# A hybrid decoder step on one core: triangular inverse in 64-blocks, an unlooped TensorE queue, and a reordered recurrence front

## The chip, the cores and the metric

One NeuronCore of a Trainium2 chip. The metric is the time of the whole program on the device, in microseconds, median of several executions. Five engines work side by side: TensorE (PE; PEld is its weight load), VectorE (DVE), ScalarE (ACT), GpSimd (POOL) and SyncE (SP, which issues DMAs). Each runs its own list of instructions in order and waits on semaphores for the others.

## What is computed

One layer step for a prompt of 512 tokens and 8 sampled tokens (520 columns in all), width 2048. Everything is fp32.

```python
xn = rms_norm(x, norm_w)
z  = xn @ w_in                       # 2048 x 8384: r, k, v, two LoRA inputs, gate | q, k, v, gate
# group A, 16 RWKV-7 heads of 64
zs = zs + mu * (zs_prev - zs)        # token shift
w  = exp(-exp(-0.5) * sigmoid(w0 + tanh(wd) @ w_up));  a = sigmoid(a0 + ad @ a_up)
kk = k * k_k / max(|k * k_k|, eps);  k = k * (1 + (a - 1) * k_a)
S_t = S_{t-1} diag(w_t) - (S_{t-1} kk_t) (kk_t a_t)^T + v_t k_t^T;   y_t = S_t r_t
y  = group_norm(y) + sum(r * k * r_k) * v       # the last term is the bonus
# group B, 16 heads of 64: QK-norm, ALiBi, three dilated windows merged by their denominators
out = x + concat(y * silu(g_r), o_att * silu(g_a)) @ w_out
```

For the prompt the recurrence is done in chunks of 128 tokens. Within a chunk it needs the inverse of a unit lower triangular 128x128 matrix I + N for each head, which is built by doubling: the inverse of 2x2 blocks, then 4x4, up to 128x128.

## The kernel before

**Stages.** A start (norm, transposes, LoRA inputs, the projection of pair 0), then 8 passes of `pair_a` (two RWKV heads each, pairs 0 to 7), 8 passes of `pair_b` (two attention heads each), then 8 passes of the output projection. While a pass works on its heads, TensorE also multiplies the input projection of the next pass: 64 *units* of six matmuls with 260 columns (`multiply_unit`, L443), 4 output tiles of 16 units. The tables `BEHIND_A` and `BEHIND_B` say after which step how many units are put into TensorE's queue (`fill`); `spread` gives the last step what is left over. The weights of a projection pass come in 8 half-tiles (8 units each): SP loads one, ScalarE rounds it (`round_half`, L419), GpSimd subtracts to get the rest (`rest_half`, L427), and unit u waits, where u is a multiple of 8, for half-tile u/8. ScalarE and GpSimd issue rounding and rest of half-tile k+1 at the unit 8k+1, at that unit's place in their own order of steps.

**Order.** Each engine's order is written by hand, as a list of named steps (`Steps`); a wait names a step of another engine. On TensorE, `pair_a` and `pair_b` are loops over seven passes, with the last pass written out behind the loop; the output passes 1 to 7 are a loop too.

**The front of `pair_a`.** TensorE: `lora` (L760), `kk` (sum of squares, L766), `tail` (transposes of the last columns, L770), `bonus` (L776), `vec` (L784), then the chunk products `g00` to `g31` (L793). The bonus waits for VectorE's `prod` (L1543) and for ScalarE's copy of the tail (L1194), whose PSUM bank it reuses. VectorE: `ssm` (reads `kk` from PSUM, L1516), four scans of the log decay (L1522), differences up to `gl` (L1533), `t1`, `kp`, `prod` (L1538 to L1543), then the products with the exponentials. ScalarE: sigmoids (L1173 to L1177), Ln and Exp of the norm (L1184, L1186), then E1, E2 (L1188, L1189), two small ones and the tail copy. GpSimd multiplies the gate (L644).

**The inverse.** `blocks_of_two` (VectorE, L1575 to L1584) makes X, the inverse of the 2x2 blocks, and its transpose XT, for 4 chunks x 2 heads = 8 matrices of 128x128. GpSimd makes a masked copy of N for each level (L653). Level l of 1 to 5 then is, for all 8 matrices, in two halves a and b:

```python
QT = nm_l^T-product with XT        # qt, L859, evicted by ScalarE (a, L1226) and VectorE (b, L1597)
X -= QT^T X                        # dx, L883, subtracted by VectorE (L1604)
XT = transpose(X)                  # tr, L895, evicted by ScalarE (a) and VectorE (b, L1611)
```

with one unit behind each of the two halves of `tr`. Level 6 works on the 64x64 quarters (L862, L886). After the inverse, four chunk steps (`rhs`, `u`, `s`, `y`) carry the state, and group norm ends the pass. The attention pass and the output pass are not touched but for the loops.

Of the kernel before, what the change touches and what calls it, by code (L numbers as in the profile page):

```python
# [140 lines left out]
class Arena:  # L141
# [3 lines left out]
    def take(self, *shape):  # L145
# [6 lines left out]
        elif len(shape) == 3:  # L152
# [10 lines left out]
BEHIND_A = {"lora": 4, "kk": 3, "tail": 3, "bonus": 8, "vec": 1, "g21": 1, "tokb": 3, "nn23": 1, "bcast": 3,  # L163
            **{f"tr{l}{h}": 1 for l in LV for h in "ab" if l < LEVELS - 1}, "qt6b": 1, "dx6b": 1,
# [30 lines left out]
def build(nc, x_prompt, x_sample, state_wkv, state_shift, cache_k, cache_v, norm_w, w_in, mu_shift,  # L195
# [18 lines left out]
    with ExitStack() as ctx:  # L214
# [23 lines left out]
        def bc(a, n):  # L238
# [122 lines left out]
                      *[f"{s}{l}{h}" for l in LV for s in ("qt", "dx", "tr") for h in "ab"  # L361
                        if (l, s) != (last, "tr")],
                      *[f"{s}{c}" for c in range(NC) for s in ("rhs", "u", "s", "y")],
                      "st", "mean", "var"])
        ACT_A = Steps(["ksq", "sgw", "sga", "sgg", "ln", "rn", "e1", "e2", "g", "dcs", "tail", "vec",
                       "nn01", "tokb", "tokk", "tokv", "nn23", "rv",
                       *[f"{s}{l}" for l in LV for s in ("qt", "tr") if (l, s) != (last, "tr")],
# [3 lines left out]
        DVE_A = Steps(["gnp", "ssm", "scan", "lcm", "lc0", "gl0", "gl", "t1", "kp", "prod",  # L371
                       "kk", "at", "kka", "rt", "bt", "kt", "bon",
                       "g00", "g01", "g10", "g11", "g20", "g21", "xma", "xa", "xtma", "xta",
                       "g30", "g31", "xmb", "xb", "xtmb", "xtb",
                       *[f"{s}{l}" for l in LV for s in ("qt", "xa", "xb", "tr")
                         if (l, s) != (last, "tr")],
# [96 lines left out]


# [156 lines left out]
        def _(pool):  # L631
# [7 lines left out]
            def pair_a(i, g, ahead=True):  # L639
# [7 lines left out]
                for l in range(1, last):  # L647
                    if l == 1:
                        pool.wait_ge(a_act, ACT_A.at(i, "nn23"))
                        pool.wait_ge(a_dve, DVE_A.at(i, "bt"))  # L650
                    elif l > 2:
                        pool.wait_ge(a_pe, PE_A.at(i, f"qt{l - 2}b"))
# [5 lines left out]
                    if l > 1:  # L658
                        for s in ("qt", "dx", "tr"):
                            for h in "ab":  # L660
                                feed(f"{s}{l - 1}{h}")
                for name in PE_A.names[PE_A.index[f"qt{last - 1}a"]:]:
                    feed(name)
# [39 lines left out]
        def _(pe):  # L703
# [42 lines left out]
            def pair_a(i, g):  # L746
# [91 lines left out]
                for l in LV:  # L838
                    nm = NM[(l - 1) % 2]
                    for h in range(2):  # L840
                        hn = "ab"[h]
                        bank = (3, 0)[h]
                        if h == 0:
                            if l < last:
                                pe.wait_ge(a_pool, POOL_A.at(i, f"nm{l}"))
                            if l == 1:
                                pe.wait_ge(a_dve, DVE_A.at(i, "xtb"))
                                pe.wait_ge(a_act, ACT_A.at(i, "nn23"))
                            else:
                                pe.wait_ge(a_act, ACT_A.at(i, f"tr{l - 1}"))  # L850
                        elif l == 1:
                            pe.wait_ge(a_act, ACT_A.at(i, "rv"))
                        else:
                            pe.wait_ge(a_dve, DVE_A.at(i, f"tr{l - 1}"))
                        if l == last:
                            pe.sem_inc(s_passed, 1)
                        for q in range(4):
                            if l < last:
                                mm = pe.matmul(HB[:, bank, q * C:(q + 1) * C], nm[:, 4 * h + q, :],  # L859
                                               XT[:, 4 * h + q, :], start=True, stop=True)  # L860
                            else:
                                mm = pe.matmul(HB[0:64, bank, q * 64:(q + 1) * 64], NN[64:128, 4 * h + q, 0:64],  # L862
                                               XT[64:128, 4 * h + q, 64:128], start=True, stop=True)
# [960 lines left out]
```

## Time and profile before

| | |
|---|---|
| runs | 1683.51 us median of 3 (1681.51 to 1683.93) |
| profiled execution | 1678.24 us, its span 1676.4 us |
| mean granted TensorE clock | 0.972 of full speed |
| TensorE's share of the chain that ended last | 80%, then VectorE 8%, "issue" 6% |
| VectorE, ScalarE, GpSimd busy | 48%, 34%, 32% |

In rows of the trace a line begins with the source line, the engine and the operation, then the tiles written and read, the shapes and the count. "Idle before" is the time that the engine stood still ahead of the group, and the arrow names what ended it. One fp32 product in the program is two MATMUL instructions; a matmul of the projection (L443, fp32r) is one.

### The profile page before, as it was taken

To read this page: it belongs to the slowest core of one execution; us is meant where nothing else is said; L and a number is where in the kernel's file an instruction comes from. 1 tells how busy PE (TensorE), PEld (TensorE's weight loads), DVE (VectorE), ACT (ScalarE), POOL (GpSimd) and SP (SyncE) were. 2 spreads that over 40 slices of the span, in tenths; PEclk is the share of its full clock that TensorE was granted. 3 is DMA by queue.
4 is the path that set the end of the run, shared out by engine and by line. 5 is a ranking of instruction groups with operands and counts; after the bars stand their busy time and mean duration, and the time that the engine had idled before them with its cause. 6 is when DMAs were issued, how large, how long until landed. Compare 5 with 4: busy or idle time off the path is not lost.

```text
span 1676.4 us, 32674 instructions
## 1 busy us (share of the span) xinstructions
PE 1554.7 (93%) x12509; PEld 1452.1 (87%) x12509; DVE 798.2 (48%) x1301; ACT 565.6 (34%) x927; POOL 532.0 (32%) x256
## 2 busy tenths in 40 slices
PE   5999989989899898999998989999999999679998
PEld 4988978979889798898897988998998998579998
DVE  3236474564655746556466534534535535430000
ACT  5242242322422424224232243443443443422221
POOL 0334123232232322322324223333333333443332
PEclk9999999999999999999999999999999999799999
DMA  6321130310302203004031064464563563425542
GB/s 192 84 80 26 30 96 1 87 39 7 105 14 65 60 1 99 26 9 116 1 83 52 26 157 101 123 144 94 125 145 92 128 144 91 150 77 151 144 117 79
DMA packets 249819, 140.88 MB, mean 84 GB/s; under 512 B 11053, under 2 KB 242798, under 8 KB 249198
## 3 DMA queue, kind: packets, MB, share of 16 engines
q1 hardware_dynamic: 228156, 126.23, 29.3%
q10 hardware_dynamic: 21570, 13.23, 2.6%
q8 instruction: 81, 1.33, 0.3%
q14 instruction: 12, 0.10, 0.0%
HBM read 124.11 MB, written 15.26 MB: 83 GB/s over the span
## 4 chain that ended last, share of the span: by engine, by line
PE 80%; DVE 8%; issue 6%; ACT 2%; DMA 2%; SPq 1%; POOL 1%; DVEq 0%; ACTq 0%; POOLq 0%
PE acc L443 50%; PE head_banks L859 5%; PE head_banks L883 5%; PE head_banks L895 2%; DVE AREN L1522 2%; PE head_banks L1016 1%; DVE AREN L1584 1%; PE head_banks L793 1%; PE head_banks L1036 1%; DVE AREN L1748 1%; PE head_banks L760 1%; PE head_banks L1029 1%; PE head_banks L911 1%; PE head_banks L920 1%; PE head_banks L776 1%
## 5 line engine op out<-in xcount | busy, mean ns | idle before, releaser
L427 POOL TENSOR_TENSOR WL<-WR,WH 128x1024 fp32r<-128x1024 f32 (+1 forms) x164 | 399.8, 2438 | 883.1 <-ACT WH L419 874.9
L443 PE MATMUL acc<-XH,WH 128*128 128x260 f32 (+1 forms) x2624 | 586.4, 305 | 22.1 <-POOL XL L693 11.3
L443 PE MATMUL acc<-XH,WL 128*128 128x260 f32 (+1 forms) x2624 | 532.4, 285 | 0.0
L443 PE MATMUL acc<-XL,WH 128*128 128x260 f32 (+1 forms) x2624 | 532.1, 285 | 0.0
L443 PEld LDWEIGHTS acc<-XH,WH 128*128 128x128 f32 (+1 forms) x2624 | 409.3, 191 | 59.9 <-issue 31.7
L443 PEld LDWEIGHTS acc<-XL,WH 128*128 128x128 f32 (+1 forms) x2624 | 408.9, 190 | 0.0
L443 PEld LDWEIGHTS acc<-XH,WL 128*128 128x128 f32 (+1 forms) x2624 | 407.9, 190 | 0.0
L419 ACT ACTIVATE WH<-WR 128x1024 fp32r<-128x1024 f32 (+1 forms) x164 | 171.9, 1048 | 184.0 <-PE acc L443 158.8
L653 POOL TENSOR_TENSOR AREN<-AREN,CA 128x1024 f32<-128x1024 f32 x40 | 87.0, 2174 | 165.5 <-PE head_banks L859 83.1
L1226 ACT ACTIVATE AREN<-head_banks 128x512 f32<-128x512 f32 x80 | 48.0, 600 | 216.9 <-PE head_banks L895 115.0
L859 PE MATMUL head_banks<-AREN 128*128 128x128 f32 x640 | 91.2, 303 | 22.0 <-DVE AREN L1584 19.3
L859 PEld LDWEIGHTS head_banks<-AREN 128*128 128x128 f32 x640 | 87.1, 218 | 23.6 <-issue 23.6
L451 ACT ACTIVATE AREN<-acc 128x520 f32<-128x520 f32 (+1 forms) x82 | 49.3, 602 | 164.0 <-PE acc L443 163.1
L1797 DVE TENSOR_TENSOR AREN<-head_banks,AREN 128x512 f32<-128x512 f32 x16 | 11.1, 691 | 173.0 <-PE head_banks L1087 173.0
L883 PE MATMUL head_banks<-AREN 128*128 128x128 f32 x640 | 86.8, 289 | 0.0
L883 PEld LDWEIGHTS head_banks<-AREN 128*128 128x128 f32 x640 | 80.1, 197 | 1.6 <-issue 0.5
L1748 DVE CUSTOM_DVE_ANT_0 AREN<-AREN 128x128 f32<-128x128 f32 (+3 forms) x64 | 68.8, 1075 | 18.3 <-ACT AREN L1357 18.3
L1597 DVE COPY AREN<-head_banks 128x512 f32<-128x512 f32 x40 | 27.7, 693 | 88.2 <-PE head_banks L859 88.2
L1604 DVE TENSOR_TENSOR AREN<-AREN,head_banks 128x512 f32<-128x512 f32 x80 | 55.1, 689 | 24.9 <-PE head_banks L883 24.9
L1368 ACT ACTIVATE AREN<-head_banks 128x128 f32<-128x128 f32 (+3 forms) x64 | 27.9, 436 | 112.6 <-PE head_banks L1029 112.6
L1567 DVE TENSOR_TENSOR AREN<-head_banks,CA 128x512 f32<-128x512 f32 x64 | 40.4, 684 | 28.8 <-PE head_banks L793 28.6
L1735 DVE CUSTOM_DVE_ANT_0 AREN<-head_banks,AREN 128x128 f32<-128x128 f32 (+3 forms) x64 | 30.7, 488 | 42.0 <-PE head_banks L1016 41.4
(232 smaller groups left out, 1778.6 us busy)
## 6 DMA issues: line engine op xcount, KB each, us to landing
WR<-in_w_in SPq DMA_DIRECT2D x128, 512.0 KB, 4.1
WR<-in_w_out SPq DMA_DIRECT2D x32, 512.0 KB, 5.8
out<-AREN ACTq DMA_DIRECT2D x32, 256.0 KB, 2.9
AREN<-in_cache_k_win SPq DMA_DIRECT2D x16, 384.0 KB, 8.5
AREN<-in_cache_v_win SPq DMA_DIRECT2D x16, 384.0 KB, 9.3
mix_scratch<-AREN ACTq DMA_DIRECT2D x16, 260.0 KB, 2.8
AREN<-in_x_prompt SPq DMA_DIRECT2D x4, 1024.0 KB, 8.0
AREN<-in_cache_k_win SPq DMA_DIRECT2D x8, 512.0 KB, 7.1
```

The costliest lines, as they stand in the source:

```text
L419: act.activation(WH[:, k % 2, :, 0:M], WR[:, k % 4, :, 0:M], ACT.Copy).then_inc(s_hi, 1)
L427: pool.tensor_tensor(WL[:, k % 2, :, 0:M], WR[:, k % 4, :, 0:M], WH[:, k % 2, :, 0:M].bitcast(F32), ALU.subtract).then_inc(s_lo, 1)
L443: mm = pe.matmul(acc[0:M, hf, 0:HT], w[:, k % 2, j, 0:M], x[:, kt, hf * HT:(hf + 1) * HT], start=(kt == 0 and n == 0), stop=(kt == KT - 1 ...
L451: act.activation(dst, ACC[t % 2][0:M, :, 0:HT], ACT.Copy).then_inc(s_evac, 1)
L653: pool.tensor_tensor(NM[(l - 1) % 2], NN, bc(ca[f"lev{l}"], 8), ALU.mult)\
L859: mm = pe.matmul(HB[:, bank, q * C:(q + 1) * C], nm[:, 4 * h + q, :], XT[:, 4 * h + q, :], start=True, stop=True)
L883: mm = pe.matmul(HB[:, bank, q * C:(q + 1) * C], QT[:, 4 * h + q, :], X[:, 4 * h + q, :], start=True, stop=True)
L895: mm = pe.transpose(HB[:, bank, q * C:(q + 1) * C], X[:, 4 * h + q, :], ident)
L1226: act.activation(dst, HB[:, 3, :], ACT.Copy).then_inc(a_act, ACT_A.one(f"{s}{l}"))
L1567: dve.tensor_tensor(GR[:, c, 4 * h:4 * h + 4, :].rearrange("p (s k) t -> p s k t", s=2), HB[:, bank, :].rearrange("p (s k t) -> p s k t", ...
L1604: dve.tensor_tensor(part, part, HB[:, 1 + h, :], ALU.subtract)\
L1748: dve.tensor_tensor_reduce(out=PP[:, j % 2, 0:n], in0=EE[:, j % 2, 0:n], in1=cb["mult"][:, T - n:T], scale=1.0, scalar=0.0, op0=ALU.mult, ...
```

## The change

1. Levels 1 to 5 work on the two 64x64 diagonal blocks of each 128x128 matrix alone (elsewhere X and XT are zero until level 6). X and XT are both updated by products, so the transposes go: `dy` updates XT, `dx` updates X, and each needs only half of the columns (`half_of`). The top block lies on partitions 0 to 63 and the low one on 64 to 127 of inputs and outputs. All 8 matrices are one group; ScalarE evicts the top blocks of QT, VectorE the low ones, and VectorE does each subtraction in two instructions.
2. Units move: `bonus` 8 to 3, `tail` 3 to 5, `bcast` (ahead of level 1) 3 to 11, and each level 2 to 1.
3. TensorE's three loops are written out in Python, with constants in the waits.
4. In the front, VectorE's order becomes scans, `t1`, `kp`, `prod`, differences to `gl`, `ssm`, then `rt` and `kt` ahead of `kk`; ScalarE does E1 and E2 ahead of Ln and Exp of the norm. The tail copy stays where it was, behind these and two small exponentials.

```diff
-BEHIND_A = {"lora": 4, "kk": 3, "tail": 3, "bonus": 8, "vec": 1, "g21": 1, "tokb": 3, "nn23": 1, "bcast": 3,
-            **{f"tr{l}{h}": 1 for l in LV for h in "ab" if l < LEVELS - 1}, "qt6b": 1, "dx6b": 1,
+BEHIND_A = {"lora": 4, "kk": 3, "tail": 5, "bonus": 3, "vec": 1, "g21": 1, "tokb": 3, "nn23": 1, "bcast": 11,
+            **{f"qt{l}": 1 for l in LV if l < LEVELS - 1}, "qt6b": 1, "dx6b": 1,
...
-        ACT_A = Steps(["ksq", "sgw", "sga", "sgg", "ln", "rn", "e1", "e2", "g", "dcs", "tail", "vec",
+        ACT_A = Steps(["ksq", "sgw", "sga", "sgg", "e1", "e2", "ln", "rn", "g", "dcs", "tail", "vec",
...
+        def half_of(a, l, which):
+            m = 2 ** l
+            if len(a.shape) == 2:
+                return a.rearrange("p (n u m) -> p n u m", u=2, m=m)[:, :, which, :]
+            return a.rearrange("p q (n u m) -> p q n u m", u=2, m=m)[:, :, :, which, :]
+        def blocks_at(l):
+            top, low = slice(0, 64), slice(64, 128)
+            return ((top, 3, 1), (low, 0, 2)) if l % 2 else ((top, 1, 3), (low, 2, 0))
...
+                for l in range(1, last):
+                    blocks = blocks_at(l)
+                    pe.wait_ge(a_pool, POOL_A.at(i, f"nm{l}"))
+                    if l == 1:
+                        pe.wait_ge(a_act, ACT_A.at(i, "rv"))
+                        pe.wait_ge(a_dve, DVE_A.at(i, "xtb"))
+                    else:
+                        pe.wait_ge(a_dve, DVE_A.at(i, f"xt{l - 1}"))
+                    pe.sem_inc(s_passed, 1)
+                    for q in range(8):
+                        for k, bank, _ in blocks:
+                            mm = pe.matmul(HB[k, bank, q * 64:(q + 1) * 64], nm[k, q, k], XT[k, q, k],
+                                           start=True, stop=True)
+                    mm.then_inc(a_pe, PE_A.one(f"qt{l}"))
+                    fill(f"qt{l}")
+                    pe.wait_ge(a_act, ACT_A.at(i, f"qt{l}"))
+                    pe.wait_ge(a_dve, DVE_A.at(i, f"qt{l}"))
+                    pe.sem_inc(s_passed, 1)
+                    for q in range(8):
+                        for k, _, bank in blocks:
+                            mm = pe.matmul(HB[k, bank, q * 32:(q + 1) * 32], X[k, q, k],
+                                           half_of(QT[k, q, k], l, 1), start=True, stop=True)
+                    mm.then_inc(a_pe, PE_A.one(f"dy{l}"))
+                    fill(f"dy{l}")
+                    for q in range(8):
+                        for k, bank, _ in blocks:
+                            mm = pe.matmul(HB[k, bank, q * 32:(q + 1) * 32], QT[k, q, k],
+                                           half_of(X[k, q, k], l, 0), start=True, stop=True)
+                    mm.then_inc(a_pe, PE_A.one(f"dx{l}"))
+                    fill(f"dx{l}")
...
-            with pe.Fori(0, PAIRS - 1) as i:
+            for i in range(0, PAIRS - 1):
...
+                act.wait_ge(a_dve, DVE_A.at(i, "gl"))
+                act.activation(E1, LC, ACT.Exp, scale=-DEC).then_inc(a_act, ACT_A.one("e1"))
+                act.activation(E2, LC, ACT.Exp, scale=DEC).then_inc(a_act, ACT_A.one("e2"))
                 act.wait_ge(a_dve, DVE_A.at(i, "ssm"))
                 act.activation(SSM, SSM, ACT.Ln, scale=float(2 ** LNS)).then_inc(a_act, ACT_A.one("ln"))
                 act.wait_ge(a_act, ACT_A.at(i, "ln"))
                 act.activation(RN, SSM, ACT.Exp, scale=-0.5, bias=ln_back).then_inc(a_act, ACT_A.one("rn"))
-                act.wait_ge(a_dve, DVE_A.at(i, "gl"))
-                act.activation(E1, LC, ACT.Exp, scale=-DEC).then_inc(a_act, ACT_A.one("e1"))
-                act.activation(E2, LC, ACT.Exp, scale=DEC).then_inc(a_act, ACT_A.one("e2"))
...
+                for l in range(1, last):
+                    act.wait_ge(a_pe, PE_A.at(i, f"qt{l}"))
+                    act.activation(QT[0:64, :, 0:64], HB[0:64, blocks_at(l)[0][1], :].rearrange("p (q t) -> p q t", q=8), ACT.Copy)\
+                       .then_inc(a_act, ACT_A.one(f"qt{l}"))
+                    for s in ("qt", "dy", "dx"):
...
-        DVE_A = Steps(["gnp", "ssm", "scan", "lcm", "lc0", "gl0", "gl", "t1", "kp", "prod",
-                       "kk", "at", "kka", "rt", "bt", "kt", "bon",
+        DVE_A = Steps(["gnp", "scan", "t1", "kp", "prod", "lcm", "lc0", "gl0", "gl", "ssm",
+                       "rt", "kt", "kk", "at", "kka", "bt", "bon",
...
+                    for name, step, dst, which in (("dy", "xt", XT, 1), ("dx", "x", X, 0)):
+                        dve.wait_ge(a_pe, PE_A.at(i, f"{name}{l}"))
+                        for k, bank_x, bank_t in blocks_at(l):
+                            part = half_of(dst[k, :, k], l, which)
+                            sub = dve.tensor_tensor(part, part, HB[k, bank_t if which else bank_x, 0:256]
+                                                    .rearrange("p (q n m) -> p q n m", q=8, m=2 ** l), ALU.subtract)
```

## Rows read from the trace of the kernel before

**Rows 1.** page, part 1: TensorE's busy time, share of the span and instructions

```profile
PE 1554.7 (93%) x12509; PEld 1452.1 (87%) x12509; DVE 798.2 (48%) x1301; ACT 565.6 (34%) x927; POOL 532.0 (32%) x256
```

**Rows 2.** waits of TensorE: us in total, times, longest

```profile
PE head_banks L859 <- DVE AREN L1584: 19.3, 7, 2.8
...
PE head_banks L776 <- DVE AREN L1543: 16.7, 8, 2.7
...
PE head_banks L760 <- issue: 10.3, 6, 2.0
```

**Rows 3.** chain of waits, start and pair 1: start us, us, what

```profile
51.09 34.76 PE acc L443 x288
...
215.97 1.71 issue
...
258.66 3.56 PE head_banks L859 x16
...
266.55 1.78 PE head_banks L859 x16
...
270.73 0.72 PE acc L443 x6
...
290.76 1.07 PE head_banks L862 x16
291.83 0.92 PE acc L443 x6
```

**Rows 4.** stretches: length, busy us of PE, PEld, DVE, ACT, POOL; granted clock; DMA

```profile
215.00:228.00 13.00, 11.29 (x84) 10.59 (x82) 9.13 (x14) 8.14 (x10) 3.71 (x3) 1.00 0.27 75
228.00:236.00 8.00, 5.33 (x28) 4.88 (x27) 7.77 (x12) 2.78 (x6) 2.42 (x1) 0.79 0.23 65
...
256.00:264.00 8.00, 5.34 (x32) 5.20 (x33) 3.91 (x3) 0.60 (x1) 6.08 (x3) 0.79 0.00 0
```

**Rows 5.** timeline of TensorE, pair 1: start us, us, instructions

```profile
222.43 1.04 PE L766 MATMUL head_banks<-AREN,CA 128*128 128x260 f32 x4
...
240.59 2.00 PE L793 MATMUL head_banks<-AREN 64*128 64x256 f32 x16
...
298.14 0.45 PE L939 MATMUL head_banks<-AREN 128*64 128x128 f32 x4
298.42 0.39 PE L941 MATMUL head_banks<-AREN 128*64 128x128 f32 x4
```

**Rows 6.** groups of VectorE by shape: busy us, mean ns, idle before

```profile
L1597 DVE COPY AREN<-head_banks 128x512 f32<-128x512 f32 x40 | 27.7, 693 | 88.2 <-PE head_banks L859 88.2
...
L1607 DVE TENSOR_SCALAR AREN<-head_banks 64x256 f32<-64x256 f32 x16 | 6.7, 417 | 9.3 <-PE head_banks L886 8.9
```

**Rows 7.** timeline ahead of level 1, GpSimd and VectorE, pair 1

```profile
252.21 2.42 POOL L653 TENSOR_TENSOR AREN<-AREN,CA 128x1024 f32<-128x1024 f32 x1 [10.33 <-ACT AREN L1214]
255.11 2.87 POOL L427 TENSOR_TENSOR WL<-WR,WH 128x1024 fp32r<-128x1024 f32 x1 [0.48 <-ACT WH L419]
...
255.81 2.71 DVE L1584 TENSOR_TENSOR AREN<-CA,AREN 128x512 f32<-128x512 f32 x1
```

**Rows 8.** groups of weight loads by shape: the bonus

```profile
L776 PEld LDWEIGHTS head_banks<-AREN,CA 128*128 128x128 f32 x32 | 7.0, 241 | 19.3 <-ACT AREN L1194 16.6 <-DVE AREN L1543 1.8
```

**Rows 9.** timeline of the front, pair 7: VectorE, GpSimd, ScalarE

```profile
875.29 0.17 DVE L1514 COPY AREN<-PT 128x2 f32<-128x2 f32 x1
...
877.70 3.49 DVE L1522 TENSOR_TENSOR_SCAN AREN<-CA,AREN 128x128 f32<-128x128 f32 x4
...
882.18 0.48 DVE L1538 TENSOR_SCALAR AREN<-AREN 128x520 f32<-128x520 f32 x1
...
878.49 2.42 POOL L427 TENSOR_TENSOR WL<-WR,WH 128x1024 fp32r<-128x1024 f32 x1 [1.32 <-issue]
...
882.30 0.64 ACT L1188 ACTIVATE AREN<-AREN 128x516 f32<-128x516 f32 x1 [2.64 <-DVE AREN L1533]
...
883.56 0.46 ACT L1194 ACTIVATE AREN<-head_banks 9x384 f32<-9x384 f32 x1
```

More of the change, by code:

```diff
@@ L651, in pair_a @@
                     elif l > 2:
-                        pool.wait_ge(a_pe, PE_A.at(i, f"qt{l - 2}b"))
+                        pool.wait_ge(a_pe, PE_A.at(i, f"qt{l - 2}"))
                     pool.tensor_tensor(NM[(l - 1) % 2], NN, bc(ca[f"lev{l}"], 8), ALU.mult)\
@@ L658, in pair_a @@
                     if l > 1:
[L659 to L662, printed above, removed]
+                        for s in ("qt", "dy", "dx"):
+                            feed(f"{s}{l - 1}")
+                for name in PE_A.names[PE_A.index[f"qt{last - 1}"]:]:
                     feed(name)
@@ new lines, in pair_a @@
+                    mm.then_inc(a_pe, PE_A.one(f"dy{l}"))
[6 more added lines that the diff above has]
+                    fill(f"dx{l}")
+                for h in range(2):
+                    if h == 0:
+                        pe.wait_ge(a_dve, DVE_A.at(i, f"xt{last - 1}"))
+                        pe.sem_inc(s_passed, 1)
+                    for q in range(4):
+                        mm = pe.matmul(HB[0:64, 1 + h, q * 64:(q + 1) * 64], NN[64:128, 4 * h + q, 0:64],
+                                       XT[64:128, 4 * h + q, 64:128], start=True, stop=True)
+                    mm.then_inc(a_pe, PE_A.one(f"qt{last}{'ab'[h]}"))
+                    fill(f"qt{last}{'ab'[h]}")
@@ new lines, in pair_a @@
+                for h in range(2):
+                    if h == 0:
+                        pe.wait_ge(a_dve, DVE_A.at(i, f"x{last - 1}"))
+                        pe.wait_ge(a_act, ACT_A.at(i, f"qt{last}"))
+                    else:
+                        pe.wait_ge(a_dve, DVE_A.at(i, f"qt{last}"))
+                    pe.sem_inc(s_passed, 1)
+                    for q in range(4):
+                        mm = pe.matmul(HB[0:64, (3, 0)[h], q * 64:(q + 1) * 64], X[0:64, 4 * h + q, 0:64],
+                                       QT[0:64, 4 * h + q, 64:128], start=True, stop=True)
+                    mm.then_inc(a_pe, PE_A.one(f"dx{last}{'ab'[h]}"))
+                    fill(f"dx{last}{'ab'[h]}")
@@ L1075, in _ @@
             pe.wait_ge(a_dve, DVE_A.at(PAIRS - 1, "yc"))
-            with pe.Fori(0, PAIRS - 1) as i:
+            for i in range(0, PAIRS - 1):
                 pair_b(i, group_b(i + 1))
@@ L1104, in _ @@
             out_pair(0, first=True)
-            with pe.Fori(1, D // 256) as m:
+            for m in range(1, D // 256):
                 out_pair(m)
@@ L1524, in pair_a @@
                 scan.then_inc(a_dve, DVE_A.one("scan"))
+                dve.wait_ge(a_act, ACT_A.at(i, "sga"))
+                dve.wait_ge(o_sst, done(0, i, 16))
+                dve.tensor_scalar(T1, A_, 1.0, P_["k_a"], ALU.subtract, ALU.mult).then_inc(a_dve, DVE_A.one("t1"))
+                after("t1")
+                dve.scalar_tensor_tensor(out=KP, in0=T1, scalar=1.0, in1=M3[:, 1], op0=ALU.add, op1=ALU.mult)\
+                   .then_inc(a_dve, DVE_A.one("kp"))
+                after("kp")
+                dve.scalar_tensor_tensor(out=T1, in0=M3[:, 0], scalar=P_["r_k"], in1=KP, op0=ALU.mult, op1=ALU.mult)\
+                   .then_inc(a_dve, DVE_A.one("prod"))
                 after("scan")
```

146 lines of the change are left out of this document (32 added, 114 removed).

## The prediction

> **What bounds the kernel now.** I read the page first: TensorE is busy for 93% of the span [rows 1], so only work taken off its queue, or a hole closed in it, can show. Second the list of waits, TensorE's rows alone: three waits in the eight recurrence pairs (0 to 7) hold nearly all that the change can touch: the first level's matmul (L859) waits for VectorE's L1584, the bonus product (L776) for L1543, and L760, the first matmul of a pass, for nothing that the profile shows, six times, 10.3 us in all [rows 2]. Third the chain of waits over one pair [rows 3]. There the reader sees 1.71 us of "issue" ahead of each pass that returns through the loop, level 1 at 258.66 us taking 3.56 us for what level 2 does in 1.78 us, and between 258.66 and 290.76 us the five levels, 32.1 us, with TensorE always busy. Fourth the stretches: behind the two long waits the mean granted clock is 0.79, behind the 1.71 us hole it stays at 1.00 [rows 4]. So the limit is TensorE's own instruction count, and the waits of 2.7 to 2.8 us cost their length and then some time at 1.2 GHz.
>
> **The levels.** Before, a level is 8 products `qt`, 8 `dx` and 8 transposes of 128x128 with two units of the next projection in between (a unit, six matmuls, is 0.72 us [rows 3]). After, it is 16 products of 64x64 by 64 columns (`qt`), then twice 16 of 64x64 by 32 columns (`dy`, `dx`), no transpose, and one unit. A program matmul in fp32 is two instructions in the trace (16 instructions for 8 products), so each group has 32. Alone on the array, 16 instructions of 64x64 by 64 columns take 1.07 us [rows 3], 67 ns each. The question is whether the top and the low block, on other rows and other columns of the array, run at once. No row has both at once, but each half is there. L793 uses half the rows: 16 instructions of 256 columns take 2.00 us, 125 ns, though four of 260 columns on all rows (L766) take 1.04 us, 260 ns. L939 and L941 use half the columns: of two runs of four with 128 columns the second starts 0.28 us after the first, 70 ns each [rows 5], against 111 ns for L859 (16 in 1.78 us). So halves overlap, and I take 16 pairs of 58 to 60 ns, 0.95 us a group. The loading of 64 columns of weights may keep `dy` and `dx` at the `qt` pace though they stream half; that is in the value.
>
> One level then, counted from its first `qt`: matmuls issued by 1.0 us, results complete at about 1.15; ScalarE copies the top half, VectorE the low half, 0.69 us for 512 columns [rows 6], ready at 1.9. The unit fills that time: behind blocks it takes 0.92 us, not 0.72 (L443 behind L862 [rows 3]), so it ends at 1.95, and `dy` starts at 2.05. `dy` is complete at 3.2; VectorE subtracts two halves of 256 columns, 0.42 us each [rows 6], and the next `qt` starts at 4.15, `dx` having run meanwhile. VectorE's second pair of subtractions, 0.84 us, lies beside the next `qt` and its unit; uncovered it would cost 0.84 us a level. 5 x 4.15 = 20.75 us. The five units no longer here are done elsewhere, 5 x 0.72 = 3.6. Gain: 32.1 - 20.75 - 3.6 = 7.75 us a pair, 62 us in eight, of which 1.8 a pair is the half clock of level 1. From below: if `dy` and `dx` take half of 0.95 us, a level is 3.75 and the gain 16 us more. From above: no overlap, in the rivals. The masks that GpSimd makes for levels 3 to 5 wait for the whole `qt` two levels back, so each must fit in two levels, 8 us; one takes 2.4 us, and between the third and the fourth stands one rounding of 2.4 to 2.9 us [rows 7], which just fits.
>
> Row and rule on the switch: the row shows 0.2 us lost when full-width matmuls follow blocks [rows 3]. The Trainium skill, TensorEngine Tiling, section Tiling Modes (Key Properties), says that changing the tiling mode, not only the tile, drains TensorE, which speaks against a unit between block groups. By the rule alone one would put a whole matmul's passage at both ends of each group. By the row it is 0.2 us a level, and 0.2 is in the sum.
>
> **Ahead of the levels.** The broadcast step now carries 11 units and not 3, so eight more, 5.8 us, stand before level 1. The old wait of 2.75 us goes: VectorE's L1584 takes 2.7 us, against 0.69 us for a copy of its length from PSUM, where GpSimd works beside it on SBUF [rows 6, 7], but even if three such steps are held up they end near 261 us, and TensorE arrives near 263. What is late next is another thing: units 24 to 31 need the rounding rest of half-tile 3, which is issued on GpSimd behind the first level mask, and that waits for the last copy of `nn23`. Before, this rest was made under the bonus units. Now: mask 252.21 to 254.63, rest to 257.1 or 257.5 [rows 7], while TensorE is through three units at 255.65 (258.66 less 2.8, and a matmul's tail [rows 2, 3]). New hole 1.9 us, about as long as the loop's, which left the clock at 1.00. Gain 2.75 - 1.9 = 0.85 a pair, 6.8 us; the two ends are no hole (22 us) and a hole as before (0).
>
> **The front.** The scans and the bonus product go ahead of the norm, so VectorE has `prod` early. But L776 waits for two things, and its weight load names the other: ScalarE's L1194, the copy of the shift tail, 16.6 us [rows 8]. That copy stands in ScalarE's queue behind E1, E2, now also behind Ln and Exp of the norm, as nothing moves it. Pair 7, the last, starts without a loop hole, as all pairs will: VectorE is free at 875.46; four scans took 3.49 us with GpSimd's 2.42 us beside them, so 1.1 to 1.5 alone, and end at 877, or at 877.9 if the gate on GpSimd holds one up; t1, 0.48, and `kp`, 0.7 like other steps of that length, reach 878.2 to 879.1, where GpSimd's rounding rest, 2.42 us, gets in ahead of `prod`, so `prod` ends near 882.2; from the end of the scans to E1 was 1.1 us, so E1 starts at 883.3, not 882.30; from E1 to the end of the tail copy was 1.7 us, plus Ln and Exp, each as long as E1's 0.64, and the step between them: 886.4, not 884.02 [rows 9]. The bonus starts 2.4 us later than in that pair; TensorE has two more units before it (1.44 us), a hole of some 2.3 us stays, and three units fewer are done before the next step. Against pair 7 that loses 0.9 us; against a looped pair, whose bonus also ran into the half clock, it gains up to 0.8. I take 0 for all eight. The ends are -10 and +19 us, the latter if the hole of 2.35 us really goes eight times. Moving E1 and E2 ahead of Ln costs nothing by itself, since VectorE fills the time with `rt` and `kt`; without these it is their 1.4 us.
>
> **No loops on TensorE.** Six holes of 1.71 us go: 10.3 us [rows 2, 3]. In the attention and output passes no such hole is listed, so nothing is gained there. Straight code is not slower: 288 matmuls of the unlooped start run in 34.76 us without a break [rows 3]. If each of the 14 returns there cost one such hole instead, that would be 24 us.
>
> **Sum.** 62 + 6.8 + 0 + 10.3 = 79.1 us. The profiled execution took 1678.24 us (span 1676.4): 1599. The median of the runs is 5.3 us above it: **1604**.
>
> **Rivals.**
> *Half clock in the levels (slower).* The blocks light two quarters of the array at a time, and no row here shows the clock under such work for longer than 1 us. If the chip takes that for rest, as it took the two long waits, the level stage runs at 1.2 GHz, where level 1 cost twice [rows 3]: three groups of 1.9 us and a unit of 1.85 make 7.6 us a level, 3.45 more. With four of five levels slow that is 13.8 us a pair: 1714. From three slow levels on it eats the whole gain. For it: the wait at L776 sufficed. Against: TensorE is never without work for more than 0.2 us there.
> *No overlap (slower).* Each block as alone: three groups of 2.14 us and a unit make 7.4 us a level, 130 us more: 1734. Rows 5 speak against it twice. The Trainium skill, TensorE: Matmul & The Clock Gate, Part 1 ("Wait — 56ns, not 53.3ns?"), names about 62 ns of sequencer time per matmul where hardware decode is off; by it, as an estimate, 96 block matmuls take 6 us, a level near 6.9 and the time near 1714.
> *The front clears and the levels run at 3.75 us.* 19 + 16 us less: 1569.
> *The change doesn't do what it says*: the front rival in reverse is already my forecast, since the bonus stays late.
>
> **Chances.** Forecast 0.67, its own range 1578 to 1632; faster front or levels 0.09; half clock 0.16, a third of it with only one or two slow levels (1630 to 1675); no overlap 0.04; the rest, 0.04, near no change. The range 1565 to 1675 leaves out about 2 in 10. About 0.2% is what runs of this kernel can tell apart: faster 0.80, within 0.2% 0.03, slower 0.17.
>
> **What would show it.** Levels: `qt1` to `qt6` near 21 us, start of the low block's matmul within some 10 ns of the top's. Broadcast: L443 waiting 1 to 2 us for GpSimd's L427. Front: the weight load of the bonus still waiting for ScalarE's tail copy. Loop: no "issue" ahead of L760's successor. I am wrong if the granted clock falls in the levels, or if the bonus starts without a wait.

## The result, and the profile after

The changed kernel takes 1582.31 us (median of 4 runs, 1582.08 to 1584.89) where the kernel before takes 1682.51 on the same chip (1678.61 to 1683.93): ratio 0.9411, 95% interval 0.9392 to 0.9431. That is 100 us gained. The forecast was 79 us gained and a time of 1604; the measured time lies inside its range of 1565 to 1675. The control run e5, with nine runs of the kernel before, has 96.4 us (1678.56 to 1582.14).

Where it came from shows when each recurrence pair is cut at the starts of four TensorE instructions in the timeline: its first matmul, the first gram, `qt1` and `qt6`. Sums in us over the eight pairs (the last stage over seven), worked out from the profiled executions; the runs of the next section stand beside them:

```
                         front    grams to qt1   qt1 to qt6   qt6 to next pair
before                  176.96       144.51        258.71         252.49
after                   151.55       182.43        165.03         240.97
units moved, 0.72 each  -17.3        +46.1         -28.8             0
change net of units      -8.1         -8.2         -64.9          -11.5
e1  loops back          145.77       182.53        167.43         252.15
e2  old front order     157.05       187.37        165.09         240.83
e3  old units           184.90       150.74        165.13         240.81
e9  new levels alone    179.63       150.73        167.30         252.38
e10 bare levels         151.44       211.46        207.81         271.89
```

The four net sums make 92.7 us of the 93.3 by which the spans differ (1676.4 and 1583.1). The other 7 us between the medians are the choice of execution: the profiled one lay 4.3 us below the median of before and 2.6 above that of after.

Page of the kernel after, part 1; TensorE lost 74.6 us of work against [rows 1] and is as busy in share as before:

```profile
PE 1480.1 (93%) x14749; PEld 1368.4 (86%) x14749; DVE 792.9 (50%) x1341; ACT 541.4 (34%) x887; POOL 536.3 (34%) x256
```

Its waits, TensorE's rows (total, times, longest). Of the three of [rows 2], the first level no longer waits and the loop's hole is gone; the bonus (L787) still waits, now for the tail copy and at most 1.5 us. The projection's units wait for GpSimd's rest (L427), in the pairs twice each: 0.9 us ahead of the bonus and 1.5 us ahead of level 1:

```profile
PE acc L443 <- POOL WL L427: 27.1, 20, 3.4
...
PE head_banks L787 <- ACT AREN L1197: 11.4, 8, 1.5
...
PE head_banks L804 <- DVE AREN L1567: 4.1, 8, 0.5
```

The chain of waits of pair 1, against [rows 3]: start us, length us, what.

```profile
240.54 2.82 POOL WL L427
243.36 0.04 issue
243.40 6.01 PE acc L443 x48
249.41 1.08 PE head_banks L861 x32
250.49 0.91 PE acc L443 x6
251.40 1.05 PE head_banks L870 x32
252.45 0.93 PE head_banks L876 x32
253.39 0.07 issue
253.45 1.15 PE head_banks L861 x32
```

GpSimd's timeline has the mask L665 from 238.16 to 240.57, and the rest follows it; TensorE's units from 243.40 on follow the end of the rest. In TensorE's timeline that is idle time of 1.54 us:

```profile
238.16 2.41 POOL L665 TENSOR_TENSOR AREN<-AREN,CA 128x1024 f32<-128x1024 f32 x1 [10.93 <-ACT AREN L1217]
...
243.40 0.51 PE L443 MATMUL acc<-XH,WH 128*128 128x260 f32 x2 [1.54 <-POOL WL L427]
```

From its first matmul to that of the next, a level takes 4.11 us in TensorE's timeline (249.34 to 253.45 in this pair), the last of the five some 4.17, with TensorE at work throughout.

VectorE's groups by shape (busy us, mean ns), to [rows 6]: the copy of 512 columns and the subtraction of 256 cost what the rows of before said.

```profile
L1601 DVE TENSOR_TENSOR AREN<-AREN,head_banks 64x256 f32<-64x256 f32 x160 | 67.1, 419 | 55.6 <-PE head_banks L870 51.3
...
L1595 DVE COPY AREN<-head_banks 64x512 f32<-64x512 f32 x40 | 27.8, 695 | 42.0 <-PE head_banks L861 42.0
```

Stretches of pair 2, to [rows 4]: length, busy us (instructions) of PE, PEld, DVE, ACT, POOL, then granted clock, DMA share, GB/s. The first is the front, the second the levels; both run at 1.00, that is 2.4 GHz:

```profile
316.00:324.00 8.00, 6.52 (x52) 5.90 (x52) 4.92 (x8) 4.92 (x10) 2.37 (x1) 1.00 0.21 61
...
344.00:355.00 11.00, 10.87 (x243) 10.16 (x243) 4.47 (x10) 2.74 (x4) 5.31 (x3) 1.00 0.01 3
```

Timelines of the same front (pair 2 starts at 304.40), one engine after the other, to [rows 8, 9]: GpSimd's rest beside `prod` (L1529), E1, the tail copy, the bonus that waits for it, and GpSimd's next rest.

```profile
311.44 2.72 POOL L427 TENSOR_TENSOR WL<-WR,WH 128x1024 fp32r<-128x1024 f32 x1 [1.23 <-ACT WH L419]
...
311.96 2.75 DVE L1529 SCALAR_TENSOR_TENSOR AREN<-AREN 128x520 f32<-128x520 f32 x1
...
315.68 0.64 ACT L1187 ACTIVATE AREN<-AREN 128x516 f32<-128x516 f32 x1 [4.33 <-DVE AREN L1539]
...
318.24 0.47 ACT L1197 ACTIVATE AREN<-head_banks 9x384 f32<-9x384 f32 x1
...
318.85 1.12 PE L787 MATMUL head_banks<-AREN,CA 128*128 128x260 f32 x4 [1.48 <-ACT AREN L1197]
...
321.54 2.37 POOL L427 TENSOR_TENSOR WL<-WR,WH 128x1024 fp32r<-128x1024 f32 x1 [7.38 <-ACT WH L419]
```

### The profile page after: what moved, and what is told of

Same layout as the page of the kernel before. It is cut to its first block, busy times and chain, and to the rows that moved or that the text cites. A ratio compares the mean times of both kernels' runs of the same rounds, so it can differ in the third digit from the quotient of the medians.

```text
span 1583.1 us, 36273 instructions
## 1 busy us (share of the span) xinstructions
PE 1480.1 (93%) x14749; PEld 1368.4 (86%) x14749; DVE 792.9 (50%) x1341; ACT 541.4 (34%) x887; POOL 536.3 (34%) x256
## 4 chain that ended last, share of the span: by engine, by line
PE 73%; DVE 8%; issue 8%; ACT 4%; POOL 3%; DMA 1%; SPq 1%; DVEq 0%; ACTq 0%; POOLq 0%
PE acc L443 49%; PE head_banks L861 3%; PE head_banks L870 3%; PE head_banks L876 2%; POOL WL L427 2%; PE head_banks L1019 1%; PE head_banks L1039 1%; DVE AREN L1744 1%; PE head_banks L804 1%; DVE AREN L1519 1%; DVE AREN L1502 1%; PE head_banks L1032 1%; PE head_banks L914 1%; PE head_banks L923 1%; PE head_banks L988 1%
## 5 line engine op out<-in xcount | busy, mean ns | idle before, releaser
L427 POOL TENSOR_TENSOR WL<-WR,WH 128x1024 fp32r<-128x1024 f32 (+1 forms) x164 | 404.6, 2470 | 854.0 <-ACT WH L419 842.8
L443 PE MATMUL acc<-XH,WH 128*128 128x260 f32 (+1 forms) x2624 | 581.5, 303 | 38.8 <-POOL WL L427 27.1
L665 POOL TENSOR_TENSOR AREN<-AREN,CA 128x1024 f32<-128x1024 f32 x40 | 86.7, 2175 | 105.5 <-ACT AREN L1217 89.3
L1601 DVE TENSOR_TENSOR AREN<-AREN,head_banks 64x256 f32<-64x256 f32 x160 | 67.1, 419 | 55.6 <-PE head_banks L870 51.3
L1226 ACT ACTIVATE AREN<-head_banks 64x512 f32<-64x512 f32 x40 | 23.8, 596 | 108.8 <-PE head_banks L861 108.8
L1595 DVE COPY AREN<-head_banks 64x512 f32<-64x512 f32 x40 | 27.8, 695 | 42.0 <-PE head_banks L861 42.0
L861 PE MATMUL head_banks<-AREN 64*64 64x64 f32 x1280 | 45.9, 220 | 2.1
L861 PEld LDWEIGHTS head_banks<-AREN 64*64 64x64 f32 x1280 | 41.4, 134 | 5.8 <-issue 0.2
L1238 ACT ACTIVATE AREN<-head_banks 128x128 f32<-128x128 f32 x32 | 9.0, 280 | 108.8 <-PE head_banks L914 108.8
L870 PEld LDWEIGHTS head_banks<-AREN 64*64 64x64 f32 x1280 | 40.5, 134 | 5.5
```

The source lines that it names most:

```text
L427: pool.tensor_tensor(WL[:, k % 2, :, 0:M], WR[:, k % 4, :, 0:M], WH[:, k % 2, :, 0:M].bitcast(F32), ALU.subtract).then_inc(s_lo, 1)
L443: mm = pe.matmul(acc[0:M, hf, 0:HT], w[:, k % 2, j, 0:M], x[:, kt, hf * HT:(hf + 1) * HT], start=(kt == 0 and n == 0), stop=(kt == KT - 1 ...
L665: pool.tensor_tensor(NM[(l - 1) % 2], NN, bc(ca[f"lev{l}"], 8), ALU.mult)\
L861: mm = pe.matmul(HB[k, bank, q * 64:(q + 1) * 64], nm[k, q, k], XT[k, q, k], start=True, stop=True)
L870: mm = pe.matmul(HB[k, bank, q * 32:(q + 1) * 32], X[k, q, k], half_of(QT[k, q, k], l, 1), start=True, stop=True)
L1601: sub = dve.tensor_tensor(part, part, HB[k, bank_t if which else bank_x, 0:256] .rearrange("p (q n m) -> p q n m", q=8, m=2 ** l), ALU.sub ...
```

## The experiments

Medians of five runs and ratios to the kernel before on the same chip, where it took 1678.5 to 1680.1 us. Against the changed kernel they are read from the control, e5, which ran on another chip than e1 to e4 (the kernel before took 1678.56 and 1678.52 us on the two).

**e5, control: the changed kernel as it is.**

> The changed kernel itself, unaltered, as the measure for the other runs of this chip: ratio to the kernel before 0.940 to 0.943. If the cost of the loops in e1 (0.9482) and of the old order in e2 (0.9480) is as it seemed, both stand 0.5 to 0.8% above this one.

1582.14 us, ratio 0.9422 (0.9409 to 0.9435), as expected.

**e1, TensorE's loops back.**

```diff
-            for i in range(0, PAIRS - 1):
+            with pe.Fori(0, PAIRS - 1) as i:
...
```

The attention and the output loop go back in the same way.

> The changed kernel with TensorE's three loops back (recurrence pairs 0 to 6, attention pairs, output passes); all else as changed. Theory A: each of the seven loop starts in the recurrence costs the hole of 1.71 us that rows 3 show, the attention and output loops cost nothing (their passes kept their length, 63.07 to 62.98 us and 12.09 us both), and the granted clock stays at full: 1582 + 10 to 12 = 1592 to 1594 us. Rival B: it was the loops that let the clock fall in the front of each pair, so with them the front's 1.7 us a pair goes as well: 1604 to 1606 us, and spells of half clock in the front. Rival C: the loops cost nothing of their own: 1580 to 1585.

1592.09 us, ratio 0.9482 (0.9469 to 0.9495), 10.0 us over the control: theory A's price, though not its place. The stage with the loop start is 11.2 us longer and the levels 2.4, but the front is 5.7 us shorter: the other engines run on through the loop's hole, and the bonus waits 6.3 us in all for the tail copy, not 11.4. Theory B is out by its time, but not wholly by its mechanism: in two of the eight pairs the clock fell for a short spell, 1.5 and 0.2 us behind the loop's hole (of 1.9 and 1.8 us).

**e2, the old front order in the changed kernel.** VectorE does `ssm` first, `kt` behind `bt`; ScalarE Ln and Exp ahead of E1 and E2.

```diff
-        DVE_A = Steps(["gnp", "scan", "t1", "kp", "prod", "lcm", "lc0", "gl0", "gl", "ssm",
-                       "rt", "kt", "kk", "at", "kka", "bt", "bon",
+        DVE_A = Steps(["gnp", "ssm", "scan", "lcm", "lc0", "gl0", "gl", "t1", "kp", "prod",
+                       "kk", "at", "kka", "rt", "bt", "kt", "bon",
...
```

> The changed kernel with VectorE's and ScalarE's instructions of the front in the order of the kernel before (norm first, logarithm ahead of the exponentials); units as changed (5 ahead of the bonus product). Theory A, clock: the front gained 1.7 us a pair because the hole ahead of the bonus fell from 2.67 us to 1.48 and the clock no longer fell to half behind it; the old order ends product and tail copy 13.0 and 12.8 us behind the pair's start, where TensorE comes at 13.0, so its hole is under 0.7 us, the clock stays, and the grams start 0 to 0.7 us later than now by the bonus product on VectorE: 1580 to 1589 us. Rival B, order: the new order is what made the front shorter, 1.7 us a pair: 1595 to 1598 us.

1592.62 us, ratio 0.9480 (0.9467 to 0.9493), 10.5 us over the control, between both. The bonus waits 0.2 us, as worked out under A; the price falls at the grams. `kt` (L1560), the last of VectorE's products in this order, stands beside GpSimd's second rest and takes 2.86 us in place of 0.69; the grams then wait 2.0 us for what follows it, and in five pairs the clock falls behind that. TensorE's wait, VectorE's and GpSimd's timeline and a stretch of TensorE's clock:

```profile
PE head_banks L804 <- DVE AREN L1562: 15.9, 8, 2.0
```

```profile
323.77 2.86 DVE L1560 TENSOR_TENSOR AREN<-AREN 128x512 f32<-128x512 f32 x1
326.55 0.69 DVE L1562 TENSOR_TENSOR AREN<-head_banks,AREN 128x520 f32<-128x520 f32 x1
...
323.15 2.93 POOL L427 TENSOR_TENSOR WL<-WR,WH 128x1024 fp32r<-128x1024 f32 x1 [5.94 <-ACT WH L419]
```

```profile
326.00:334.00 8.00, 6.65 (x40) 4.75 (x42) 5.10 (x8) 0.60 (x1) 0.08 (x1) 0.79 0.24 68
```

So the order is worth 10 us, and not by the early bonus product: it keeps VectorE's products out of GpSimd's way. Two things do that at once. `kt` moves to an earlier place, and the tail copy moves to a later one, with the rounding and the rest behind it: in e2 (pair from 307.65) the copy ends 12.7 us and the rest starts 15.5 us behind the first matmul, in the changed kernel 14.3 and 17.1, when the products are through. Which of the two counts is not separated; e6 (below), which moves the copy alone, loses in the same way.

**e3, the units of before (3, 8, and 8 behind the broadcast).**

```diff
-"tail": 5, "bonus": 3, ... "bcast": 11,
+"tail": 3, "bonus": 8, ... "bcast": 8,
```

> The changed kernel with 3, 8 and 8 units behind the tail, the bonus and the broadcast, where it has 5, 3 and 11 (the kernel before had 3, 8 and 3). The bonus wait starts 1.44 us earlier, so its hole is 2.9 us; three units leave the broadcast, and the fourth half-tile is asked for behind the bonus, so the hole of 1.5 to 2.1 us at the broadcast goes. Theory A, clock: a hole of 2.9 us lets the granted clock fall to half for some 3.4 us, which costs 1.7 us a pair (half-clock bonus and units): 1.44 more hole, 1.9 us less at the broadcast, 1.7 for the clock, that is +1.2 us a pair: 1588 to 1598 us. Rival B, no part of the clock: 1574 to 1583 us, and no spell at half clock in the front.

1585.86 us, ratio 0.9449 (0.9436 to 0.9462), 3.7 us over the control, between the two theories. The bonus waits 2.9 us; three of eight fronts fall to half clock (24.15 us against 22.6), and the broadcast's hole is gone. Waits and stretch:

```profile
PE head_banks L787 <- ACT AREN L1197: 22.9, 8, 2.9
```

```profile
316.00:324.00 8.00, 5.82 (x32) 5.67 (x33) 4.35 (x7) 3.06 (x7) 2.38 (x1) 0.79 0.13 37
```

Both theories had part of it: such a hole can lower the clock, but here only in three pairs of eight.

**e9, the new levels alone, in the kernel before.** Loops, front order and front units as before, 8 units behind the broadcast.

> The kernel before with the new levels alone: loops, front order and units ahead of the bonus (3 and 8) as before; the five units that the new levels have no room for stand behind the broadcast (8). Theory A, by the lengths of the other runs: front 22.3 us, grams to level 1 18.85 (five more units, three of them in the hole of 2.8 us that level 1 had), levels 20.95, the rest 36.2, so 98.3 us a pair where the kernel before has 109.2: 87 us gained, 1586 to 1597 us. Rival B, the edits add as their single reversals did (loops 10, order 10.5, units 3.7 us over the control's 1582): 1603 to 1609 us. Rival C, the forecast's own 62 us of the levels and nothing more: 1612 to 1620 us.

1597.41 us, ratio 0.9511 (0.9497 to 0.9524): 83 us of the gain, just above theory A's range. B and C fail: the levels' freed units also fill the 2.8 us in which level 1 waited (middle stage 150.73 us, 40 units more than before's 144.51). Loops, order and units together add only 15 us to that, though each costs 10.0, 10.5 and 3.7 to take back.

**e4, the two blocks one after the other.**

```diff
-                    for q in range(8):
-                        for k, bank, _ in blocks:
+                    for k, bank, _ in blocks:
+                        for q in range(8):
```

> The changed kernel with the matmuls of levels 1 to 5 ordered by block: the eight of the top block, then the eight of the lower one, where the two blocks alternate. Theory A, the two diagonal quarters of the array run beside each other only where neighbouring matmuls are of different quarters: a group of 32 instructions takes 1.9 us in place of 0.96, the rate of level 6, whose 16 instructions of one quarter take about 1.0 us; 120 groups, +115 us: 1680 to 1710 us. Rival B, the matmuls of one quarter follow each other as fast as those of two: 1580 to 1590 us.

1769.27 us (2 runs), ratio 1.0539 (1.0520 to 1.0558): 187 us over the control. Theory A holds for the groups, 1.90 us for 32 instructions where alternating ones take some 0.95 from start to start, and misses the rest: the granted clock falls in the levels and stays low, with TensorE busy for all of the stretch and without a hole of even 0.15 us ahead of the fall. The unit in each level is there as in the changed kernel. Timeline and stretches:

```profile
272.68 1.90 PE L861 MATMUL head_banks<-AREN 64*64 64x64 f32 x32
```

```profile
280.00:290.00 10.00, 10.00 (x182) 9.59 (x181) 3.91 (x8) 2.13 (x3) 6.27 (x3) 1.00 0.01 2
290.00:300.00 10.00, 10.00 (x109) 9.65 (x106) 2.58 (x6) 0.59 (x1) 0.00 (x0) 0.51 0.01 2
```

**e10, no unit inside the levels.**

```diff
-"bcast": 11, **{f"qt{l}": 1 for l in LV if l < LEVELS - 1}, ...
+"bcast": 16, ...
```

> The changed kernel with the units behind qt1 to qt5 moved to the broadcast (16 there): levels 1 to 5 without a unit of projection in them. Theory A, the unit only covers the copies of QT (0.60 us on ScalarE, 0.70 on VectorE), which the two other products wait for in any case: each of the 40 units costs its 0.72 us again at the broadcast and the level keeps about its 4.11 us: 25 to 32 us more, 1607 to 1614 us, the clock full in the levels. Rival B, clock: with a hole of 0.7 us in each level and only quarters of the array at work the granted clock falls in the levels: 20 us of levels take 28 or more, over 1640 us. Rival C, the level shortens by the unit: 1580 to 1585 us.

1689.64 us (12 runs, 1680.91 to 1697.17), ratio 1.0059 (1.0040 to 1.0078), 107.5 us over the control: theory B. Moving the units costs 29.1 us (middle stage), as A has it, and a level at full clock keeps its length (`qt1` to `qt6` 20.5 us in two pairs), with a hole of 0.84 us. But in six pairs the clock falls within the levels, in the other two right behind them, which adds 43 us there and 31 behind. Taking the unit out did two things, it took full-array work out of the level and opened the hole; which of them let the clock fall is not separated. Waits, TensorE's timeline of a level at full clock and one at half, and two stretches:

```profile
PE head_banks L870 <- DVE AREN L1595: 33.4, 40, 0.8
```

```profile
380.46 1.15 PE L861 MATMUL head_banks<-AREN 64*64 64x64 f32 x32
382.45 1.12 PE L870 MATMUL head_banks<-AREN 64*64 64x32 f32 x32 [0.84 <-DVE AREN L1595]
...
390.74 1.98 PE L861 MATMUL head_banks<-AREN 64*64 64x64 f32 x32
393.55 1.92 PE L870 MATMUL head_banks<-AREN 64*64 64x32 f32 x32 [0.83 <-DVE AREN L1595]
```

```profile
394.00:404.00 10.00, 9.17 (x172) 9.01 (x172) 3.77 (x9) 0.59 (x1) 0.79 (x1) 0.50 0.01 3
...
606.00:616.00 10.00, 7.57 (x225) 7.04 (x224) 5.34 (x11) 1.77 (x3) 6.98 (x5) 1.00 0.01 3
```

**e11, more units ahead of the bonus in the kernel before** (`"tail": 5, "bonus": 6`).

> The kernel before with one change: 5 and 6 units behind tail and bonus where it has 3 and 8. The bonus hole of 2.67 us shrinks to 1.2, the two units come off the path behind it, where grams would then wait for bon under 0.2 us. Theory A, clock: the hole is too short to let the clock fall behind it, so besides 1.4 us in each of eight pairs the 1.4 us of the pairs goes whose front lay at half clock (22.9 us against 21.5): 1678 - 12 - 6 to 11 = 1655 to 1661 us, spells of half clock in the front gone. Rival B, no part of the clock: 1665 to 1669 us. Rival C: another operation is right behind (kka or bon on VectorE), under 4 us gained: 1674 to 1678.

1663.84 us (6 runs, 1659.28 to 1669.52), ratio 0.9901 (0.9880 to 0.9923), between A and B, and inconclusive. Three runs lie at 1659 to 1660, as A has it (granted clock 0.983 to 0.986 over the span), three at 1667 to 1670, near B (0.974 to 0.981); the trace is of the longest. In it the wait at the bonus falls from 16.7 to 2.3 us in all, but a unit waits for GpSimd's rest behind it, and half clock moved to another place: in five of the six looped pairs it begins 0.1 to 1.6 us behind the first matmul, after the loop's hole. From TensorE's timeline of a pair:

```profile
669.75 0.51 PE L443 MATMUL acc<-XH,WH 128*128 128x260 f32 x2 [0.83 <-POOL WL L427]
```

What the bonus hole alone cost the kernel before is not separated.

**e6, the tail copy ahead of the exponentials.** Copy and transfers move up as they are; the next rounding still stands behind Ln and Exp.

```diff
-"sgg", "e1", "e2", "ln", "rn", "g", "dcs", "tail", "vec"
+"sgg", "tail", "e1", "e2", "ln", "rn", "g", "dcs", "vec"
...
```

> The changed kernel with ScalarE's copy of the tail rows (and the two transfers behind it) ahead of the exponentials. Theory A: the hole of 1.48 us ahead of the bonus product goes in all eight pairs, but ScalarE's rounding of the next half-tile then starts 2 us earlier (it stands behind the copy's transfers), GpSimd's difference of it runs 2 us earlier, into VectorE's kka and bt, which wait for it as rows 7 show of two such operations; the grams start late by about 1.2 us: a net gain of 0 to 0.5 us a pair, 0 to 4 us. Rival B: nothing is late next, 1.48 x 8 = 12 us gained.

1596.06 us, ratio 0.9504 (0.9489 to 0.9518): 13.9 us slower than the control. Neither theory has the time (A put it at 0 to 4 us gained, B at 12); the mechanism is A's, at a much higher price. GpSimd's rest now lies on `kka`, which takes 2.85 us; `vec` waits 2.1 us for it, and the clock falls in six of eight pairs. Waits, VectorE's and GpSimd's timeline:

```profile
PE head_banks L795 <- DVE AREN L1556: 16.2, 8, 2.1
```

```profile
321.65 2.85 DVE L1556 TENSOR_TENSOR AREN<-AREN 128x520 f32<-128x520 f32 x1
...
321.51 2.43 POOL L427 TENSOR_TENSOR WL<-WR,WH 128x1024 fp32r<-128x1024 f32 x1 [5.29 <-ACT WH L419]
```

**e7, GpSimd's fourth rest ahead of the first mask.**

```diff
                     if l == 1:
+                        feed("tokb")
                         pool.wait_ge(a_act, ACT_A.at(i, "nn23"))
...
-                        for name in ("tokb", "tokk", "tokv", "nn23", "bcast"):
+                        for name in ("tokk", "tokv", "nn23", "bcast"):
```

> The changed kernel with GpSimd's difference of the fourth half-tile ahead of the mask of level 1 (feed of tokb ahead of the wait for nn23). Theory A: the hole of 1.5 to 2.1 us at the broadcast's units goes, and the mask, which ends 0.5 us later at most, is asked for only behind the 11 units: 12 to 16 us gained of 8 pairs. Rival B: GpSimd's difference then runs beside VectorE's masked grams or the operations xma to xta and holds these up (2.7 us for one in rows 7): level 1 waits instead, 0 to 6 us gained or lost.

1570.00 us, ratio 0.9348 (0.9336 to 0.9361), 12.1 us under the control: theory A. Grams to `qt1` takes 21.0 us a pair in place of 22.8, and the units' waits for L427 fall from 27.1 us to this:

```profile
PE acc L443 <- POOL WL L427: 15.0, 12, 3.7
```

**e8, three moves: e6 with the next rounding kept behind `vec`, e7, and the pair's first rounding ahead of the table load.**

> The changed kernel with three moves: the tail copy ahead of the exponentials with the next rounding kept behind the copy of the vectors (vec), GpSimd's fourth difference ahead of the mask, and the first rounding of a pair ahead of ScalarE's table load, so that the units at GpSimd's first difference (hole 0.90 us) don't wait. Theory A: the three holes of 0.90, 1.48 and 1.5 to 2.1 us go in each of eight pairs, 3.9 to 4.5 us, less 0.5 us at the grams: 27 to 36 us under the control. Rival B: another chain is right behind (product, logarithm, kka, bon on VectorE and ScalarE), and the front ends where it ended: only the broadcast's part is gained, 10 to 16 us.

1559.16 us, ratio 0.9289 (0.9277 to 0.9302), 23 us under the control, between the two theories. The holes of 0.90 and 1.48 us and that at the broadcast are gone, but a wait of 1.3 us stands at the vectors.

**e12, e8 without the early first rounding.**

> The kernel of the three moves without the third: the first rounding of a pair again behind ScalarE's table load. Theory A, in the three moves the early rounding only moved GpSimd's difference from the bonus's product to the scans (4.41 us for the four in place of 2.24), so VectorE's chain ended where it had, and TensorE's 0.90 us came back as a wait of 1.27 us at the vectors: the same time, 1556 to 1562 us, with the hole at the first difference back and the wait at the vectors under 0.4 us. Rival B, the third move paid its 0.9 us in eight pairs: 1564 to 1568 us.

1557.81 us, ratio 0.9280 (0.9266 to 0.9294), 24 us under the control and, with e8, the fastest version here. Theory A: the third move paid nothing. In e8 GpSimd's rest met the scans, here it meets `prod`; VectorE's chain ends alike, and the unit's wait of 0.89 us for the rest is back without lengthening the pair. Scans and `prod` of e8, then of e12:

```profile
301.05 4.41 DVE L1520 TENSOR_TENSOR_SCAN AREN<-CA,AREN 128x128 f32<-128x128 f32 x4
...
306.62 0.76 DVE L1530 SCALAR_TENSOR_TENSOR AREN<-AREN 128x520 f32<-128x520 f32 x1
```

```profile
301.81 2.23 DVE L1520 TENSOR_TENSOR_SCAN AREN<-CA,AREN 128x128 f32<-128x128 f32 x4
...
305.19 2.75 DVE L1530 SCALAR_TENSOR_TENSOR AREN<-AREN 128x520 f32<-128x520 f32 x1
```

Against e7 the early tail copy with the late rounding is worth 12.2 us, near the 11.4 us that the bonus waited in all.

## Why the prediction was right, and which term was mis-sized

*Levels: 62 forecast, 64.9 measured.* Every step of the cycle stands: groups of some 0.95 us, the unit behind blocks 0.91 us, copies of 0.60 and 0.70, subtractions of 0.42, a level of 4.11 to 4.2 us against 4.15. Five levels take 20.6 us against 20.75; the rest of the 2.9 us is that two pairs of the kernel before lost more to half clock (33.3 us where pair 1 took 32.0). What sets the level is the copy of QT: `dy` starts 0.10 to 0.13 us behind the end of VectorE's copy both with the unit (changed kernel) and without it (e10, 20.5 us for five levels at full clock), so that the 0.2 us of the switch, which is in the sum, is hardly paid. e4 shows that the speed comes from the two diagonal quarters running at once. `dy` and `dx` do keep the pace of `qt`, so the bound of 3.75 us was not reached. The some 62 ns per matmul that the Trainium skill names for hardware decode switched off (TensorE: Matmul & The Clock Gate, Part 1) don't bind in this trace: the 32 instructions of `dx` start within 0.88 us, 28 ns apart in the mean. Whether decode is off here, no run shows.

*Ahead of the levels: 6.8 forecast, 8.2 measured.* The new hole, its place and its cause were right (1.54 us idle, 1.8 us a pair by e7, which takes it away; 1.9 forecast). One premise was read from pair 1 alone: that the loop's hole leaves the clock at 1.00. In pairs 4 and 6 of the same trace the clock falls 1.7 us behind the first matmul after a loop hole of 1.5 us (TensorE's timeline of pair 4, and a stretch):

```profile
546.92 2.24 PE L760 MATMUL head_banks<-AREN 96*128 96x260 f32 x8 [1.50 <-issue]
...
546.50:554.50 8.00, 7.58 (x40) 7.16 (x41) 2.88 (x6) 5.73 (x7) 2.16 (x2) 0.79 0.37 112
```

That the new hole left the clock alone in all eight pairs was therefore not given by that row.

*Loops: 10.3 forecast, 11.5 in their stage, 10.0 by e1.* Right; the attention and output passes kept their length.

*The front: 0 forecast, 8.1 measured. This is the mis-sized term.* That the bonus stays behind the tail copy was right. The step that failed is "a hole of some 2.3 us stays": the copy ended 14.31 us behind the pair's first matmul, not 15.05, and the hole is 1.48 us. "Against pair 7 that loses 0.9 us" became 21.12 - 2.16 - 18.88 = 0.1 gained (2.16 for three units), and "gains up to 0.8" became 1.7 in the four pairs whose clock had fallen behind the bonus's hole (fronts of 22.9 us), 0.3 in the two looped pairs where it had fallen behind the loop's hole instead and the bonus waited only 1.4 us (21.5), 0.6 in pair 0. No front of the changed kernel falls to half clock. That holes of the old size can lower the clock is shown by e3 (three of eight fronts) and e9 (six of eight, at 22.8 to 22.9 us each); the price that I gave the edit was that of the hole, with the clock in it only as "up to 0.8". "Moving E1 and E2 ahead of Ln costs nothing" left out the other end: with the old order GpSimd's rest meets VectorE's products, and the grams wait (e2).

*The median.* I added 5.3 us because the profiled execution of before lay so far under its median; that of after lay 2.6 us above its own. Of the 21.7 us between forecast and result this is 7.9, and chance: in the later runs the kernel before took 1678.5 to 1680.1 us, near the profiled 1678.24.

*Rivals.* "No overlap" is excluded by the 0.95 us and by e4. "Half clock in the levels" did not occur, but that TensorE "is never without work" is not reason enough: in e4 it is busy for 10.00 of 10.00 us and still falls to 1.2 GHz. e10 shows what the clock hung on: with the one full-array unit in each level, and no hole, it stays at 1.00; without the unit, and with a hole of 0.84 us, six pairs of eight fall in the levels, the other two right behind, and the gain is lost. The unit alone is not enough, as e4 has it too. So the argument against this rival did not carry it. The clock held with a unit that was there to fill the time of the copies, and that this would suffice was in part luck.

## What to carry to other kernels

A unit of full-array work that fills the hole inside a stage of small tiles can be worth far more than its own time: here 40 units of 0.72 us, moved out, cost 107 us, 29 of them their own time and the rest half clock. Before a wait is removed by moving an instruction up, follow what stands behind it in its queue: e6 lost 14 us where the same move with the next rounding held back gained 12. And edits that take the same slack don't add: three single reversals cost 24 us, all three together 15.

## What the runs showed of the hardware

- The granted clock does not follow TensorE's busy share. With one quarter of the array at work at a time it fell to 0.51 at a busy share of 1.00 (e4).
- The length of a hole alone does not decide it: in the changed kernel holes of 1.5 us ahead of the bonus and of the units before level 1 left it at 1.00 in every pair, loop holes of 1.5 us in the kernel before were followed by a fall in pairs 4 and 6 and those of 1.7 to 2.0 us in the other four were not, holes of 2.0 at the grams (e2) lowered it in five pairs of eight, of 2.1 at the vectors (e6) in six, of 2.9 at the bonus (e3) only in three.
- VectorE's operations on two SBUF operands that start beside a GpSimd rest (2.4 to 2.9 us) take 2.7 to 2.9 us in place of 0.69 to 0.76, whichever operation it meets: `prod`, `kt`, `kka`, and one scan of four (4.41 us for the group against 2.23). `prod`, `kt` and `kka` start 0.14 to 0.63 us behind the start of the rest, and each ends 0.55 to 0.56 us behind its end.
- Between two groups of blocks a full-width unit takes 0.91 us, not 0.72; so the two changes of mode, at which the Trainium skill has TensorE drain (TensorEngine Tiling, Tiling Modes, Key Properties), cost at most 0.2 us together here.
